# Four key and value blocks at the passage between two decoder layers, and router products ahead of the third tile

## The reference, cut to what matters

```python
for l in range(DEPTH):
    h, s = hgrn2_mixer(...) if l % 2 == 0 else gla_mixer(...)
    x = post_norm(x, h, ln_g[l, 0], ln_b[l, 0])
    x = post_norm(x, memory_cross_attention(x, mem_k[l], mem_v[l], w_q[l], w_o[l]), ln_g[l, 1], ln_b[l, 1])
    x = post_norm(x, grouped_moe(x, router_w, router_bias, ...), ln_g[l, 2], ln_b[l, 2])
# keys and values of the prompt's memory, for both layers, from the input alone:
kv[l] = (mem_prompt @ w_kv[l]).reshape(B, M, 2, X_HEADS, X_HEAD_DIM)
# router: 16 experts in 4 groups; best group by its two best, then the two best experts in it
scores = sigmoid(x @ router_w); sel = scores + router_bias
```

## Time and profile before

| what | us |
|---|---|
| median of 3 runs | 1354.54 |
| lowest, highest run | 1352.38, 1360.21 |
| the profiled execution, as timed | 1353.92 |
| its span in the trace | 1352.2 |
| busy in that span: PE, DVE, ACT, POOL | 1304.0 (96%), 989.2 (73%), 762.6 (56%), 203.8 (15%) |

### The profile page before, as it was taken

The page is one execution under the profiler, slowest core; times in us unless marked ns, Lnnn a source line. Parts: engine busy times, 40 slices in busy tenths (PEclk is TensorE's granted clock), DMA queues, the critical chain, the costliest instruction groups (busy, mean ns, idle before and its releaser), DMA issues.

```text
span 1352.2 us, 19380 instructions
## 1 busy us (share of the span) xinstructions
PE 1304.0 (96%) x7522; PEld 1089.3 (81%) x7522; DVE 989.2 (73%) x1064; ACT 762.6 (56%) x785; POOL 203.8 (15%) x240
## 2 busy tenths in 40 slices
PE   8999999999999999999998999999999999999995
PEld 6798997789777888888886799779776888888884
DVE  4546857682579988989985365784558989999894
ACT  4544633443425778787874363343444577778783
POOL 5300236310001000101011004310000000201110
PEclk9999999999999999999998999999999999999998
DMA  9784464455964999999996537345885699999990
GB/s 287 241 291 133 152 201 119 134 187 206 362 257 159 355 363 369 364 370 375 363 347 206 171 129 245 125 172 187 322 312 215 219 365 364 363 375 368 371 362 33
DMA packets 104305, 356.28 MB, mean 263 GB/s; under 512 B 8032, under 2 KB 34160, under 8 KB 74528
## 3 DMA queue, kind: packets, MB, share of 16 engines
q1 hardware_dynamic: 97056, 336.09, 68.5%
q0 software_dynamic: 7168, 19.08, 4.1%
HBM read 334.16 MB, written 26.75 MB: 267 GB/s over the span
## 4 chain that ended last, share of the span: by engine, by line
PE 81%; DVE 7%; DMA 4%; ACT 4%; POOL 2%; issue 2%; SPq 0%; POOLq 0%; DVEq 0%; ACTq 0%
PE ps L1970 64%; DMA att_kt<-in_cache_mem_v 2%; PE ps L2382 1%; PE ps L2017 1%; PE ps L2405 1%; PE ps L2593 1%; DVE mix_s L1663 1%; PE ps L2393 1%; PE ps L1979 1%; PE ps L1978 1%; PE ps L2097 1%; DMA raw<-in_xattn_w_kv 1%; DVE x L1397 1%; DVE x L1394 1%; PE ps L2213 1%
## 5 line engine op out<-in xcount | busy, mean ns | idle before, releaser
L1330 DVE TENSOR_TENSOR w_lo<-raw,w_hi 128x2048 fp32r<-128x2048 f32 x62 | 141.5, 2295 | 117.6 <-ACT w_hi L903 117.6
L1970 PE MATMUL ps<-w_hi,xt_hi 128*128 128x512 f32 x560 | 223.1, 398 | 2.1 <-DVE w_lo L1330 2.1
L1970 PE MATMUL ps<-w_hi,xt_lo 128*128 128x512 f32 x560 | 219.4, 392 | 0.0
L903 ACT ACTIVATE w_hi<-raw 128x2048 fp32r<-128x2048 f32 x64 | 121.8, 1914 | 134.6 <-PE ps L1970 48.3
L1970 PE MATMUL ps<-w_lo,xt_hi 128*128 128x512 f32 x496 | 193.9, 391 | 0.0
L1334 DVE TENSOR_TENSOR moe_lo<-moe_in_raw,w_hi 128x2048 fp32r<-128x2048 f32 x72 | 165.9, 2317 | 29.1 <-ACT w_hi L910 29.1
L1334 DVE TENSOR_TENSOR w_lo<-raw,w_hi 128x2048 fp32r<-128x2048 f32 x72 | 163.9, 2288 | 4.5 <-ACT w_hi L910 4.5
L910 ACT ACTIVATE w_hi<-moe_in_raw 128x2048 fp32r<-128x2048 f32 x72 | 137.7, 1920 | 41.4 <-PE ps L1970 35.3
L910 ACT ACTIVATE w_hi<-raw 128x2048 fp32r<-128x2048 f32 x72 | 137.7, 1915 | 12.7 <-PE ps L1970 12.5
L1970 PE MATMUL ps<-xt_lo,w_hi 128*128 128x320 f32 x416 | 128.5, 309 | 0.0
L1970 PE MATMUL ps<-xt_hi,w_lo 128*128 128x320 f32 x416 | 128.5, 309 | 0.0
(11 more groups left out here) (428 smaller groups left out, 2592.4 us busy)
## 6 DMA issues: line engine op xcount, KB each, us to landing
raw<-in_moe_w_gate SPq DMA_DIRECT2D x48, 1024.0 KB, 5.2
moe_in_raw<-in_moe_w_down SPq DMA_DIRECT2D x48, 1024.0 KB, 5.0
moe_in_raw<-in_moe_w_up SPq DMA_DIRECT2D x32, 1024.0 KB, 5.0
raw<-in_moe_w_up SPq DMA_DIRECT2D x32, 1024.0 KB, 5.6
raw<-in_hgrn_w_in SPq DMA_DIRECT2D x16, 1024.0 KB, 5.5
moe_in_raw<-in_moe_w_gate SPq DMA_DIRECT2D x16, 1024.0 KB, 5.5
raw<-in_moe_w_down SPq DMA_DIRECT2D x16, 1024.0 KB, 4.9
raw<-in_xattn_w_kv SPq DMA_DIRECT2D x15, 1024.0 KB, 8.4
```

The source lines that it names most:

```text
L903: nc.scalar.activation(hi_at(hi_slot(k)), raw_at(r), ACT.Copy).then_inc(w_high, 1)
L1330: nc.vector.tensor_tensor(lo_at(slot_of(k)), raw_at(slot_of(k)), hi_at(hi_slot(k)).bitcast(F32), ALU.subtract).then_inc(w_low, 1)
L1970: ins = mm(out, lhs, rhs, start=start and n == 0, stop=stop and n == 2, skip_group_check=shared)
```

## The change

The change alters the order of work and three helpers; the mathematics stays.

- **Blocks.** Four key and value blocks at the head and four at the passage, in place of six and two; x is transposed after blocks 0, 1 and 2 (2, 3 and 3 column groups).
- **Passage.** SP issues eight weight chunks ahead of the loads of x. PE does three whole blocks, then alternates the transposes of the tiles with parts of the fourth. ACT waits for the store of the block two before ahead of the copies of the third and fourth.
- **Router.** 16 router products on the first two tiles (256 columns) stand ahead of the third tile's transposes, where 20 filler products stood (4 and 8 remain); afterwards come 16 products on the third tile, its 64 columns read four times to make 256, and 8 on `xt_lo` with 320 columns.
- **Splits and small work.** POOL makes `xn_lo` of tile 0. ACT copies tile 1's transposes before the third tile's `rstd`, and splits one expert chunk instead of two ahead of the router's copy. DVE's first expert chunk is subtracted in two halves, one ahead of the routing and one behind it. The experts' weights are worked out in three pieces between the subtractions (`best_expert`, `second_expert`, `expert_weights`), `cw` moves from chunk 3 to 4, and the number of visits (`group_count`) moves behind chunk 4 of the first visit.

Sizes and helpers:

```diff
-KV_BLOCKS = (6, 2)
+KV_BLOCKS = (4, 4)
...
-X_AFTER = (1, 2, 3, 4)
+X_ROWS = ((0, 1), (2, 3, 4), (5, 6, 7), ())
...
-    out = [(3 if first else -1, "cw", 0)]
+    out = [(4 if first else -1, "cw", 0)]
...
-    n = KT // len(X_AFTER)
-    return range(X_AFTER.index(db) * n, X_AFTER.index(db) * n + n) if db in X_AFTER else ()
+    return X_ROWS[db]
```

SP:

```diff
-                    dense(done, done + NR + 1, groups)
+                    dense(done, done + 2 * KV_BLOCKS[1], groups)
...
-                    done += NR + 1
+                    done += 2 * KV_BLOCKS[1]
```

POOL:

```diff
+                    if t == 0:
+                        pool.wait_ge(mo[l]["xh"], 1)
+                        nc.gpsimd.tensor_tensor(st_moe["xn_lo"][:, 0, :], x[:, 0, :], st_moe["xn_hi"][:, 0, :].bitcast(F32), ALU.subtract).then_inc(mo[l]["xl"], 1)
```

ACT:

```diff
+                elif moe:
+                    turned(u, 1)
...
+                elif moe:
+                    rows_hi(1)
...
-                    rows_hi(1)
...
-                for j in range(2):
-                    split_expert(l, j, g0, True)
+                split_expert(l, 0, g0, True)
...
-                for j in range(2, MH):
+                for j in range(1, MH):
...
-                        if j == max(uses[0][0], 0):
+                        if j == (GU_LAST[0] if first else 0):
...
+                    if db >= BLOCKS0 + 2:
+                        act.wait_ge(kv_out[par], kv_outs(0) + 16)
...
+                    kv_block_out(BLOCKS0 + 1, 4)
+                    kv_block_out(BLOCKS0 + 2, 4)
...
-                    kv_block_out(BLOCKS0 + 1, 5)
+                    kv_block_out(BLOCKS0 + 3, 5)
```

DVE:

```diff
+            def split_half(k, half, g):
+                dve.wait_ge(w_high, at(k + 1, g, GCH))
+                ins = nc.vector.tensor_tensor(lo_at(0)[:, 2 * half:2 * half + 2, :], raw_at(0)[:, 2 * half:2 * half + 2, :],
+                                              hi_at(0)[:, 2 * half:2 * half + 2, :].bitcast(F32), ALU.subtract)
+                if half:
+                    ins.then_inc(w_low, 1)
...
-                for t in range(TILES):
+                for t in range(1, TILES):
...
-                split_expert(base, 0, g0)
+                split_half(base, 0, g0)
...
+                def group_count():
...
+                def best_expert():
...
+                    link(V_.scalar_tensor_tensor(out=m["sel"][:], in0=m["r2"][:], scalar=-2 * BIG, in1=m["sel"][:], op0=ALU.mult, op1=ALU.add))
+                def second_expert():
...
+                def expert_weights():
...
+                        if first and j == 0:
+                            expert_weights()
+                        if first and j == 4:
+                            group_count()
...
-                for j in range(1, 3):
-                    split_expert(base + j, j, g0)
+                split_half(base, 1, g0)
+                split_expert(base + 1, 1, g0)
...
+                split_expert(base + 2, 2, g0)
+                best_expert()
...
+                second_expert()
...
-                    for n in range(2):
+                    for n in range(5):
...
-                    split_ahead(BLOCKS0 + 1, groups)
+                    split_ahead(BLOCKS0 + 3, groups)
```

PE:

```diff
+            def route_two(u):
+                pe.wait_ge(rt_w, 2)
+                pe.wait_ge(xt_h, turns(u, 1) + 2)
+                for kt in range(KT):
+                    for n, w in enumerate((r_hi, r_lo)):
+                        mm(ps[0:EXPERTS, 4, 0:PROMPT], w[:, kt, :], xt_hi[:, kt, 0:PROMPT], start=kt == 0 and n == 0, stop=False, skip_group_check=True)
+            def route_third(u):
+                for kt in range(KT):
+                    for w in (r_hi, r_lo):
+                        mm(ps[0:EXPERTS, 4, PROMPT:NB].rearrange("p (a c) -> p a c", a=4), w[:, kt, :],
+                           xt_hi[:, kt, PROMPT:NT].unsqueeze(1).to_broadcast([P, 4, NT - PROMPT]), start=False, stop=False, skip_group_check=True)
+                pe.wait_ge(xt_l, turns(u, 2) + 1)
+                for kt in range(KT):
+                    ins = mm(ps[0:EXPERTS, 4, 0:NT], r_hi[:, kt, :], xt_lo[:, kt, 0:NT], start=False, stop=kt == KT - 1, skip_group_check=True)
+                ins.then_inc(rt_ps, 1)
...
+                elif q % 3 == 1:
+                    keep_busy(4, 7)
+                    route_two(u)
+                    keep_busy(8, 7)
...
-                if db == X_AFTER[0]:
+                if db == 0:
...
-                pe.wait_ge(rt_w, 2)
-                for kt in range(KT):
-                    mm(ps[0:EXPERTS, 4, 0:TILES * P], r_hi[:, kt, :], xt_hi[:, kt, :], start=kt == 0, stop=False)
-                    mm(ps[0:EXPERTS, 4, 0:TILES * P], r_lo[:, kt, :], xt_hi[:, kt, :], start=False, stop=False)
-                pe.wait_ge(xt_l, turns(3 + 3 * l, 2) + 1)
-                for kt in range(KT):
-                    ins = mm(ps[0:EXPERTS, 4, 0:TILES * P], r_hi[:, kt, :], xt_lo[:, kt, :], start=False, stop=kt == KT - 1)
-                ins.then_inc(rt_ps, 1)
+                route_third(3 + 3 * l)
...
-                    memory_chunk(db + 1, groups, 1, 0, 2)
+                    memory_chunk(db + 1, groups, 1, 0, 4)
...
+                    memory_chunk(db + 2, groups, 0, 0, 4)
+                    memory_chunk(db + 2, groups, 1, 0, 4)
+                    pe.wait_ge(evac[1], (db + 1) // 2 + 1)
...
-                    for t in range(TILES):
-                        turn_next(t)
-                    memory_chunk(db + 1, groups, 1, 2, 4)
+                    turn_next(0)
+                    memory_chunk(db + 3, groups, 0, 0, 2)
+                    turn_next(1)
+                    memory_chunk(db + 3, groups, 0, 2, 4)
+                    pe.wait_ge(evac[0], db // 2 + 2)
+                    turn_next(2)
+                    memory_chunk(db + 3, groups, 1, 0, 4)
```

38 lines of the change are left out of this document (18 added, 20 removed).

## The result

The changed kernel takes 1346.07 us (median of 8 runs) against 1357.30 us for the kernel before (median of 8 runs beside it). The ratio is 0.9926, with a 95% interval from 0.9904 to 0.9947, so 7 to 13 us less, about 10. 1344.1 was forecast, with -10.4 as the difference. The forecast stood on the median of the first three runs of the kernel before, 1354.54; with five more runs that median is 1357.30, so the difference agrees better (-10 against -10.4) than the time itself, which came out 2.0 us later than forecast and still under the 1347.8 at which the prediction let "faster" end. One of the eight runs took 4559 us and is left out of the ratio.

What follows compares the result with a forecast made beforehand. PE was busy 96% of the span, so only its waits, half clock and filler could be won. Head +0.4, passage -7.15 and router -3.6 sum to -10.4 us, giving 1344.1 from the median 1354.54; range 1340.5 to 1349.5.

Steps and rivals of the forecast that it cites:

- Moved work: Two blocks, 22.6 us of products, go from head to passage at full clock in both: net nothing.
- Head: Up to layer 0: waits of 1.03 us go, one of 1.4 us comes, +0.4 us (bounds -1.0 and +1.9).
- The step on chunk 3: Head: six transposes, 0.64 us, ahead of chunk 3 fill PE's first wait of 0.68 us.
- The new wait of 1.4 us for chunk 7: Head: PE waits 1.4 us for its last chunk, held by a store taken to land in 8.3 us.
- Passage: Between the layers: 4.80 us of waiting for x and 2.35 us at half clock go, -7.15 us (bounds -7.15 and -6.15).
- my three signs of being wrong: Wrong if PE waits over 3 us at head, x ends a wait, or clock under 1.00 at 400 to 440 us.
- Router stage: Last norm to first expert product: chain gains 2.1 us, 1.8 kept per layer (bounds 0.5 and 2.1), 3.6 in both.
- a step of my sum that failed: First expert visit: `group_count` needs 1.1 us and ends a good 1 us ahead of the first "down" product.
- rival four: Router stage: narrow products bring PE to half clock, 26 us more, 1370, slower than before; chance 0.04.
- One: Router stage: DVE's chunks come no earlier, so 2.1 us shrink to 0.5 per layer; -7.8, 1346.7; chance 0.15.
- Two: Passage: x takes 13 us instead of 6.6, PE idles 2.7 us, 2.35 may be lost; 1349.1; chance 0.12.
- Three: Router stage: POOL's new subtraction meets a DVE step at 409.18, 2 x 2.3 us worse, 1348.7; chance 0.03.

Runs made afterwards that it cites:

- e1: The change's key and value blocks alone, with the router stage of the kernel before: 1350.94 us, ratio 0.9953 to the kernel before.
- e3: Changed kernel with the loads of x queued ahead of the passage's last weight chunk instead of behind it: 1346.04 us, ratio 0.9927 to the kernel before.
- e12: Kernel before with 30 filler products in its wait for the next x, nothing else changed: 1355.68 us, ratio 0.9981 to the kernel before.
- e7: Changed kernel with the loads of x put behind one more weight chunk on SP's queue: 1353.20 us, ratio 0.9981 to the kernel before.
- e10: Changed kernel with x loaded ahead of the last passage chunk and the first expert pick ahead of the gathered-row steps: 1346.07 us, ratio 0.9916 to the kernel before.
- e9: Changed kernel with DVE's small steps whole again, the group count right behind the slots: 1346.74 us, ratio 0.9922 to the kernel before.
- e4: Kernel before with 20 filler products in its wait for the next x, nothing else changed: 1353.91 us, ratio 0.9983 to the kernel before.
- e5: Changed kernel with the second expert split again ahead of the router copy: 1349.32 us, ratio 0.9946 to the kernel before.
- Both parts alone: The change without its router stage, and the change without its blocks, as two kernels: 1350.94 and 1353.00 us, ratios 0.9953 and 0.9968 to the kernel before.

## Why the prediction was right, point by point

**Moved work** was to net nothing. It did: the head lost 22.90 us, and the two blocks came back at full clock. In the four traces with six blocks the head was 71.2 to 73.2 us long, in the ten with four 48.7 to 51.4; the means differ by 22.3 us, against the 22.6 of the two blocks.

**Head, +0.4 us forecast, -0.3 in the pair, +0.3 over all traces.** Layer 0 was to start near 60.9 and started at 60.62. The step on chunk 3 failed: six transposes ahead of it were to fill its 0.68 us, and it waited 0.91 us. In e1 and e3, with the same order, it waited under 0.3 us, so this is scatter of the early loads, by which heads with one order differ by up to 2 us. The new wait of 1.4 us for chunk 7 was mis-sized: the store landed in 7.2 us, not 8.3, beside the copy of the memory rows, and no trace with four blocks has a wait there.

**Passage, -7.15 us forecast, -6.9 in the pair** (15.7 us more for 22.6 us of moved products; with the head's -0.3 that is the -7.2). PE was to want x 33.9 us behind the last expert product, and did. x was to be 3.7 us early and was 0.26 late: the step that failed is the landing of 6.6 us "as before", taken from a row with a single store beside it. The last chunk (1 MB) went just ahead of x, and 9.8 us passed. The bound that I had set (9.8, "the slowest store") was the value, and it left 0.5 us to spare only on paper, since the loads were issued 0.4 us later than worked out. So one of my three signs of being wrong, x as what ends a wait, did come, with 0.26 us instead of 4.80. Chunk 8 was to be ready with under 1 us to spare; PE came to it without a wait. The half clock belonged to the wait, as forecast; e12 shows it without any change of data (2.15 us by its transposes, 4.69 to 2.54, where I had 2.35), e7 by bringing it back.

**Router stage, -1.8 us a layer forecast, -1.3 and -1.1 in the traces.** The copy of the router's result came 2.1 us sooner, as worked out, and so did the first expert products. DVE idled 2.04 us (1.8 forecast). The term that was mis-sized is what is given back after that: 0.8 to 1.0 us instead of 0.3. Two pieces of it can be read. The first is a chain that I had not looked at. The experts' combination weights now come one chunk later, and behind them stand ACT's table load, the activation and DVE's product, on which PE's transposes wait. ACT, DVE and PE of the changed kernel:

```profile
421.67 1.28 ACT L1274 ACT_TABLE_LOAD   x1
422.96 0.60 ACT L1274 ACTIVATE moe_sil<-ps 128x512 f32<-128x512 f32 x1
...
423.60 0.75 DVE L1938 SCALAR_TENSOR_TENSOR moe_h<-moe_sil,moe_cw,ps 128x512 f32<-128x512 f32 x1 [0.23 <-ACT moe_sil L1274]
...
424.40 0.39 PE L2643 MATMUL ps<-ident,moe_h 128*128 128x128 f32 x1
```

DVE is done at 424.35 and PE goes on at 424.40; before, DVE was done at 446.44, 2.0 us ahead of PE (448.41). Counted from the first expert product that is 0.4 us in layer 0 (17.66 against 17.28) and 0.55 in layer 1, and most of what e10 brought back it brought here (17.52 in both).

The second is a step of my sum that failed. `group_count` was to end 1 us ahead of the first "down" product. It ended in time itself, at 430.89, but `moe_ht_lo`, which that product waits for, stands behind it. DVE and PE:

```profile
430.75 0.14 DVE L1905 CAST n_last<-moe_mc 1x1 int32<-1x1 f32 x1
430.82 0.67 DVE L1943 TENSOR_TENSOR moe_ht_lo<-ps,moe_ht_hi 128x512 fp32r<-128x512 f32 x1
...
431.22 0.40 PE L2004 MATMUL ps<-moe_hi,xt_lo 128*128 128x512 f32 x1
431.55 0.50 PE L2004 MATMUL ps<-w_hi,moe_ht_hi 128*128 128x512 f32 x1
431.89 0.40 PE L2004 MATMUL ps<-w_lo,moe_ht_hi 128*128 128x512 f32 x1
```

`moe_ht_lo` is done at 431.49, 0.06 us ahead of PE, where the kernel before had 3.4 us to spare. PE's two steps take 0.67 us instead of 0.46, and 0.74 in layer 1, so 0.2 and 0.3 us. e9, in which the count stands behind the slots again, has 1.0 us to spare here and PE's steps at 0.23. Some 0.2 us a layer stay open, in steps too small for a row of idle time.

**What I had not priced** is the clock of the router stage. My rival four had it fall because of the change. It fell without the change: in the ten router stages whose wait was 1.5 to 1.75 us (two each in the traces of before, e1, e4, e5 and e12) it fell five times. The trace from which I predicted had it in neither layer. The change ended that by making the wait 0.57 (none in 16). Both parts alone raise the mean clock by 0.0016 and 0.0017, so the whole by an estimated 0.0033, worth 3.6 us at 1.09 for each 0.001; e3, the whole but for the order of x, has 0.0037. The sum by stages is then +0.3 (head), -4.5 (the wait for x), -2.4 (two router stages) and -3.6 (clock), -10.2; measured -10. My -10.4 reached that with one clock term of 2.35 us and a router term that was 1.2 us too large (3.6 against 2.4). The total is right partly by luck, because these two offset each other.

**Rivals.** One (VectorE eats the router's gain) is half true: 0.8 to 1.0 of 2.1 us. Two (x late) came only as 0.26 us of waiting instead of its 2.7, and e7 shows its price. Three did not occur where the change put its step, though the two engines do exclude each other elsewhere in these traces. Four did not occur.

## What to carry to other kernels

A load's landing time is read beside its future company, not its present one; give what the next layer hangs on a place in the queue ahead of a bulk chunk that waits for its slot. An idle time on the matmul engine can cost more than itself, because the clock may fall with it: here it did at 12 of 23 waits of 1.5 to 2.1 us at two places, at 4 of 4 of 1.9 to 4.8 us at a third, and at none of 26 of up to 0.6 us at the same places. So count the waits of a microsecond and more in the program, and try products whose result nobody reads in those that can't be removed. Small steps that are moved to a later gap of an engine are to be checked against what stands behind them in its queue, not only against their own deadline. A single pair of traces says little of a change under 1%: compare stage by stage, and check the mean clock of all runs before reading a difference of spans.

## What the runs showed of the hardware that was not expected

The scatter of this kernel's time, 1351 to 1363 us, is for the most part that of the granted clock: r is -0.80 to -0.93 between time and mean clock in the three sets of runs of the kernel before. The clock fell around the end of a wait, from 2.3 us before PE took up work again (before, at the passage) to 1.5 us after it (e12, at 419.99), stood at its lower level for 3.4 us, mostly with PE fully busy, and did so behind some waits of 1.5 to 2.1 us and not behind others of the same length. The same loads of x in the same order took 5.7 us in one execution and 8.4 in another. A GpSimd subtraction of 128 x 1024 took 2.38 us while DVE read the result banks, and DVE's instructions beside it kept their durations; but a GpSimd step of 0.31 us took 2.37 beside a DVE subtraction with both inputs in SBUF.
